# A hybrid decoder layer: the output projection of a tile placed inside the index work of the next

## The reference, cut to what matters

```python
scores = sum_h w_idx[h] * relu(q_idx[h] @ k_idx.T)      # 8 index heads
sel    = top_k(scores where valid, 256)                 # per query
att    = softmax(q @ k[sel].T / 8) @ v[sel]             # 8 heads of 64, 2 key/value heads
mo     = softmax(q_mem @ mem_k.T / 8) @ mem_v           # 4 heads, 256 memory tokens
o      = concat(att * silu(g_att), conv * silu(g_conv), mo * silu(g_mem)) @ w_out
y      = x + rms_norm(o, g_post)
```

## Time and profile before

| what | us |
|---|---|
| median of 3 runs | 2714.32 (2706.91 to 2717.56) |
| the profiled execution | 2714.81 |
| its span | 2712.7 |
| stage B, tiles 0 to 15 | 729.7 to 2453.1 |
| tile 10, whole | 1701.2 to 1841.7 |

### The profile page before, as it was taken

How to read it: one execution, slowest core, us unless ns; L and a number is a source line. 1 busy time by engine, 2 the same in 40 slices (tenths; PEclk the granted TensorE clock), 3 DMA queues, 4 the chain that set the end, 5 groups by cost and what they waited for, 6 DMA issues and landing times.

```text
span 2712.7 us, 34490 instructions
## 1 busy us (share of the span) xinstructions
PE 2246.7 (83%) x12592; PEld 1777.6 (66%) x12592; DVE 1414.5 (52%) x3260; ACT 1022.6 (38%) x1849; POOL 318.7 (12%) x847
## 2 busy tenths in 40 slices
PE   7999999999487887977978678687878879898865
PEld 5777777777365665765766657475766668687762
DVE  2444444442445566287487566847673645133580
ACT  1111101110244464374574655556536544352000
POOL 0000000000012121122111111201101110001004
PEclk9999999998677677678888788778977978998556
DMA  6111111110511111011011010101000101113001
GB/s 254 64 71 68 60 56 69 64 54 22 188 49 57 55 57 49 10 55 49 11 55 33 24 49 9 49 8 33 9 18 24 34 8 34 49 63 132 2 1 32
DMA packets 58412, 137.56 MB, mean 51 GB/s; under 512 B 13904, under 2 KB 26872, under 8 KB 57248
## 3 DMA queue, kind: packets, MB, share of 16 engines
q1 hardware_dynamic: 56096, 125.25, 13.7%
q0 software_dynamic: 2176, 10.49, 1.2%
HBM read 96.82 MB, written 38.90 MB: 50 GB/s over the span
## 4 chain that ended last, share of the span: by engine, by line
PE 60%; DVE 18%; ACT 10%; issue 7%; DMA 2%; POOL 1%; SPq 1%; PEld 1%; DVEq 0%; ACTq 0%; POOLq 0%; PEldq 0%
PE psum L564 12%; PE psum L1273 9%; PE psum L1262 9%; PE psum L597 8%; PE psum L1254 5%; PE psum L1231 4%; DVE sb_sc L996 4%; PE psum L1244 4%; ACT sb_ajunk L898 4%; DVE sb_junk L1011 2%; PE psum L1220 2%; ACT sb_ptb L892 2%; ACT sb_p L952 1%; PE psum L611 1%; PE psum L1706 1%
## 5 line engine op out<-in xcount | busy, mean ns | idle before, releaser
L1262 PE MATMUL psum<-sb_v,sb_ptb 128*128 128x64 f32 x2176 | 335.2, 303 | 30.7 <-ACT sb_ptb L892 29.9
L1262 PEld LDWEIGHTS psum<-sb_v,sb_ptb 128*128 128x128 f32 x2176 | 321.1, 224 | 48.8 <-ACT sb_ptb L892 48.3
L564 PE MATMUL psum<-sb_w,sb_xt 128*128 128x512 f32 (+5 forms) x1088 | 324.7, 459 | 0.5 <-DVE sb_xt L380 0.5
L1011 DVE TENSOR_SCALAR_CACHE_REDUCE sb_junk<-sb_sc,sb_c 128x384 bf16<-128x384 f32 (+6 forms) x217 | 305.6, 1408 | 4.2 <-DVE sb_mix L1190 1.0
L1244 PE MATMUL psum<-sb_ks,sb_qa 128*128 128x512 f32 (+3 forms) x640 | 204.4, 458 | 119.4 <-ACT sb_p L942 77.0
L1254 PE MATMUL psum<-sb_con,sb_p 128*128 128x128 f32 x1280 | 250.4, 327 | 63.9 <-ACT sb_p L952 41.2
L898 ACT ACTIVATE sb_ajunk<-sb_sc,sb_an 128x512 int8<-128x512 f32 (+6 forms) x217 | 293.8, 1354 | 10.3 <-POOL sb_an L826 9.8
L892 ACT ACTIVATE sb_ptb<-psum 128x512 f32<-128x512 f32 (+3 forms) x352 | 182.9, 534 | 239.3 <-PE psum L1254 237.9
L1273 PE MATMUL psum<-sb_wo,sb_mix 128*128 128x512 f32 x512 | 258.5, 669 | 13.4 <-DVEq L1193 13.4
L564 PEld LDWEIGHTS psum<-sb_w,sb_xt 128*128 128x128 f32 (+1 forms) x1088 | 178.5, 185 | 134.5 <-issue 125.1
L1231 PEld LDWEIGHTS psum<-sb_qa,sb_w 128*128 128x128 f32 x2048 | 244.2, 192 | 12.1 <-issue 4.7
(11 more groups left out here) (340 smaller groups left out, 2490.3 us busy)
## 6 DMA issues: line engine op xcount, KB each, us to landing
qt_s<-sb_qt SPq DMA_DIRECT2D x32, 512.0 KB, 2.8
sb_x<-in_x_prompt SPq DMA_DIRECT2D x16, 512.0 KB, 3.7
xt_s<-sb_xt SPq DMA_DIRECT2D x16, 512.0 KB, 2.6
sb_qa<-xt_s SPq DMA_DIRECT2D x16, 512.0 KB, 3.3
sb_qa<-qt_s SPq DMA_DIRECT2D x16, 512.0 KB, 3.5
sb_qa<-qt_s SPq DMA_DIRECT2D x32, 256.0 KB, 4.7
sb_xres<-in_x_prompt SPq DMA_DIRECT2D x16, 512.0 KB, 4.8
out_y_prompt<-sb_y SPq DMA_DIRECT2D x16, 512.0 KB, 3.4
```

The source lines that it names most:

```text
L564: mm = pe.matmul(out, m.xt[:, p, k, 0:n], m.w1[:, k, lo:hi], start=(k == 0), stop=(k == KD - 1))
L1011: return dve.tensor_scalar(m.junk[:, 0:w], m.sc(i), least[:], 0.0, ALU.is_ge, ALU.add, accum_out=m.cnt[:])
L1262: mm = pe.matmul(o, m.ptb[:, g, x * P:(x + 1) * P], v, start=st, stop=sp)
```

## The change

A tile's index stretch becomes a list of 12 segments on each engine, and the loop runs one pass longer. Segments 0 to 7 hold one gate block each, those of the second half first. Segment 7 holds the transposes of the attention of the tile before (`ta`) and the memory scores; segments 8 to 11 hold the projection of the tile before in four quarters, bank 1 first; segment 10 also holds the scores of the tile's first head. The index pairs are spread over segments 0 to 10.

On ACT both halves of the gate's input are copied to SBUF (`z0`, `z1`) beside the exponentials; the logarithm and the second exponential follow in segment 7, behind `gated` of the tile before; the memory exponentials stand ahead of the relus of segment 8. In the heads the exponential of head h + 1 stands after the second take of head h, and probes after the takes.

On DVE the division of the attention opens the next tile's list. The select of an odd tile is cut in three (segments 2, 4, 5), that of an even tile in three too (heads 5 to 7). Of the searches in a tile with index work, 2 (even j) or 7 (odd j) stand in the segments and the rest in the heads. The projection is read bank by bank: ACT squares each half, DVE multiplies each half by `gpost` (`gains`), and the scale and the residual follow in one instruction on DVE in head 2 (`residual`); POOL's addition is gone. The rows `junk` and `equal`, the latter a source of the sum in `select`, become 8-bit. `xt2` has its own buffer; `m.r` lies in a part of `p`.

On SP the second index tile's queries are issued after half of the gate weights, and the queries of a tile right behind the last scores of the tile before.

The core of the diff (of the loops, only what stands there after):

```diff
 AHEAD = 4
-Y_AFTER = 3
+SEGS = 12
+GATE_ORDER = (4, 5, 6, 7, 0, 1, 2, 3)
...
+def units(j, x):
+
+    if not searched(j + AHEAD):
+        return []
+    every = [(c, hp) for c in chunks(width(j + AHEAD), 512) for hp in range(4)]
+    return [u for k, u in enumerate(every) if k * (SEG_SCORE + 1) // len(every) == x]
...
+def searches_early(j):
+
+    return (2 if j % 2 == 0 else 7) if searched(j + AHEAD) else (4 if j % 2 == 0 else 8)
+
+
+def due(x, n):
+
+    return (x + 1) * n // SEG_SCORE > x * n // SEG_SCORE if x < SEG_SCORE else False
...
+    def load_xt(j):
+        if j >= 1:
+            sp.wait_ge(s.t_done, turns.of[("z", j - 1, 0)][1])
+        sp.dma_start(m.xt2.rearrange("p k n -> p (k n)"), io.xt_s[j]).then_inc(s.xt2_ld, 16)
+
     load_idx(FIRST)
-    for k in range(KD):
-        w = io.w_in[0, k * P:(k + 1) * P, :]
-        sp.dma_start(m.w2[:, k, 0:512], w[:, W2A[0]:W2A[1]]).then_inc(s.w_ld[k], 16)
-        sp.dma_start(m.w2[:, k, 512:1024], w[:, W2B[0]:W2B[1]]).then_inc(s.w_ld[k], 16)
+    load_xt(0)
+    for x, (lo, hi) in ((1, W2B), (0, W2A)):
+        for k in range(KD):
+            sp.dma_start(m.w2[:, k, 512 * x:512 * x + 512], io.w_in[0, k * P:(k + 1) * P, lo:hi]
+                         ).then_inc((s.w_ld, s.w_ldb)[x][k], 16)
+        if x == 1:
+            load_idx(FIRST + 1)
+    load_q(m.qa, 0, 0, s.qa_ld)
...
+        for x in range(SEGS):
+            if 0 <= j < NT and x == SEG_MEM + 1:
+                slot = scores.of[("M", j)][0]
+                act.wait_ge(s.mmax, j + 1)
+                for h in range(NMH):
+                    ins = act.activation(m.pm[:, h * 256:(h + 1) * 256], m.score2(slot)[:, mem_at(h) * 256:][:, 0:256],
+                                         ACT.Exp, bias=m.mnb[:, mem_at(h):mem_at(h) + 1], scale=SCALE,
+                                         accum_out=m.ml[:, h:h + 1])
+                ins.then_inc(s.mem_exp, 1)
+            for c, hp in units(j, x):
+                relu(j + AHEAD, c, hp)
+            if not 0 <= j < NT:
+                continue
+            if x == 3:
+                slot, n, _, _ = turns.of[("z", j, 1)]
+                act.wait_ge(s.t_done, n)
+                if j >= 1:
+                    act.wait_ge(s.gsum, j)
+                    act.wait_ge(s.t_dve, turns.of[("to", j - 1)][3])
+                act.activation(m.z1[:], m.turn[slot][:], ACT.Copy)
+                act.activation(m.gate[:, 512:768], m.turn[slot][:, 256:512], ACT.Exp, scale=-1.0).then_inc(s.zact, 1)
+            if x == SEG_MEM:
+                slot, n, _, _ = turns.of[("z", j, 0)]
+                act.wait_ge(s.t_done, n)
+                if j >= 1:
+                    act.wait_ge(s.gated, j)
+                act.activation(m.z0[:], m.turn[slot][:], ACT.Copy)
+                act.activation(m.gate[:, 0:512], m.turn[slot][:], ACT.Exp, scale=-1.0).then_inc(s.zact, 1)
+                act.wait_ge(s.zact, 2 * j + 2)
+                act.activation(m.gate[:], m.gate[:], ACT.Ln, bias=m.ones[:]).then_inc(s.zln, 1)
+                act.wait_ge(s.zln, 2 * j + 1)
+                act.activation(m.gate[:], m.gate[:], ACT.Exp, scale=-1.0).then_inc(s.zln, 1)
+            if its and due(x, probes_early(j)):
+                probe(j, its[done])
+                done += 1
+        if j >= 1:
+            square(j - 1, 1)
+            square(j - 1, 0)
+        if not 0 <= j < NT:
             continue
         for x in range(2):
             take_group(("tm", j, x))
+        exponent(j, 0)
         start = done
         for h in range(NH):
+            parts = chunks(width(j), 512)
+            for x, c in enumerate(parts):
+                take_group(("t", j, h, c))
+                if x == min(1, len(parts) - 1) and h + 1 < NH:
+                    exponent(j, h + 1)
             upto = start + (len(its) - start) * (h + 1) // NH
...
+    def select(i, c, part):
+        bias, e, run = m.bias[:, i % 2, 0:w], m.equal[:, 0:w], sc[:, 0:w // 2].bitcast(BF16)
+        if part == 0:
+            ch.inc(dve.tensor_scalar(c[:], c[:], sign, None, ALU.mult))
+            ch.link(dve.tensor_scalar(sc, sc, sign, None, ALU.mult))
+            ch.link(dve.tensor_scalar(bias, sc, c[:], 0.0, ALU.is_gt, ALU.add, accum_out=m.cnt[:]))
+            ch.inc(dve.tensor_scalar(m.more[:], m.cnt[:], -float(TOPK), None, ALU.add))
+            ch.link(dve.tensor_scalar(e, sc, c[:], None, ALU.is_equal))
+        if part == 1:
+            ch.link(dve.tensor_tensor_scan(run, e, m.one[:].to_broadcast([P, w]), m.more[:], ALU.add, ALU.min))
+        if part == 2:
+            ch.link(dve.scalar_tensor_tensor(out=e, in0=run, scalar=0.0, in1=e, op0=ALU.is_le, op1=ALU.mult))
+            ch.link(dve.tensor_tensor(bias, bias, e, ALU.add))
+            ch.link(dve.tensor_scalar(bias, bias, 1.0, MASK, ALU.subtract, ALU.mult))
...
+        half = slice(512 * x, 512 * x + 512)
+        dve.tensor_tensor(m.y[:, half], m.ybank[:, half], m.gpost[:, half], ALU.mult).then_inc(s.y_norm, 1)
...
+        dve.scalar_tensor_tensor(out=m.y[:], in0=m.y[:], scalar=m.yrs[:], in1=m.xres[:], op0=ALU.mult,
+                                 op1=ALU.add).then_inc(s.y_sum, 1)
...
+        if j >= 1:
+            attended(j - 1)
+        for x in range(SEGS):
+            acc = [(j + AHEAD, c, 2 * hp + e) for c, hp in units(j, x) for e in range(2)]
+            if d is not None and due(x, searches_early(j)):
+                search(d, done, acc)
+                done += 1
+            else:
+                for a in acc:
+                    accumulate(*a)
+            if j < 0:
+                continue
+            if j % 2 == 0 and 1 <= n < NPAIR:
+                if x == 0:
+                    exact(2 * n + 1)
+                if x in (2, 4, 5):
+                    select(2 * n + 1, m.cf, (2, 4, 5).index(x))
+            if j >= 1 and x == SEG_MEM:
+                gated(j - 1)
+                if j == NT:
+                    decode = c_prepare(dve, m, s)
+            if j == NT:
+                continue
+            if x == SEG_MEM:
+                slot, num, _, _ = scores.of[("M", j)]
+                dve.wait_ge(s.s_done, num)
+                ch.link(dve.tensor_reduce(m.mmx[:], m.score2(slot).rearrange("p (h n) -> p h n", h=NMH), AX, ALU.max))
+                dve.tensor_scalar(m.mnb[:], m.mmx[:], -SCALE, None, ALU.mult).then_inc(s.mmax, 1)
+            if x == SEG_MEM + 2:
+                dve.wait_ge(s.zln, 2 * j + 2)
+                ch.inc(dve.tensor_tensor(m.gate[:, 0:512], m.z0[:], m.gate[:, 0:512], ALU.mult))
+                ch.link(dve.tensor_tensor(m.gate[:, 512:768], m.z1[:, 256:512], m.gate[:, 512:768], ALU.mult))
+                dve.sem_inc(s.gsum, 1)
+            if x == SEG_SCORE:
+                for part in range(3):
+                    mask(j, 0, part)
...
+        for h in range(1, NH):
+            heads = 4 if j % 2 == 1 else NH - 1
+            target = min(upto, start + ((upto - start) * h + heads - 1) // heads)
...
+                if j >= 1:
+                    residual(j - 1)
...
+            if h >= 5 and d is not None and j % 2 == 1:
+                select(d, m.c, h - 5)
...
+    for j in range(FIRST - AHEAD, NT + 1):
         i = j + AHEAD
+        if searched(i):
             pe.wait_ge(s.qi_ld, 48 * (i + 1 - FIRST))
+        for x in range(SEGS):
+            if 0 <= j < NT and x < 8:
+                if x == 0:
                     pe.wait_ge(s.xt2_ld, 16 * (j + 1))
+                gate_block(j, GATE_ORDER[x])
+            if j >= 1 and x == SEG_TURN:
+                pe.wait_ge(s.att, j)
+                turn_group(("ta", j - 1), m.att, 0, 4)
+            if j >= 1 and x >= 8:
+                if x == 8:
+                    pe.wait_ge(s.cm_ld, 16 * j)
+                    pe.wait_ge(s.t_dve, turns.of[("to", j - 1)][3])
+                    if j == 1:
+                        pe.wait_ge(s.wo_ld, 32)
+                if x == 9:
+                    pe.wait_ge(s.gated, j)
+                mm = project_out(1 if x < 10 else 0, x % 2 == 0)
+                if x % 2 == 1:
+                    mm.then_inc(s.y_done, 1)
+            for c, hp in units(j, x):
+                index_pair(i, c, hp)
+            if 0 <= j < NT and x == SEG_MEM:
+                memory_scores(j)
+            if 0 <= j < NT and x == SEG_SCORE:
+                pe.wait_ge(s.qa_ld, 48 * (j + 1))
+                for h in range(first_scores(j)):
+                    scores_of(j, h)
...
-            m.r = sb(b, "r", [P, 2, 512])
-            m.junk = sb(b, "junk", [P, SEQ], BF16)
+            m.junk = sb(b, "junk", [P, SEQ], mybir.dt.uint8)
...
+            m.r = m.p[:, 1, 1024:2048].rearrange("p (e n) -> p e n", e=2)
...
+            m.xt2 = sb(b, "xt2", [P, KD, P])
+            m.gate = sb(b, "gate", [P, 768])
+            m.z0, m.z1 = sb(b, "z0", [P, 512]), sb(b, "z1", [P, 512])
+            m.equal = m.z0[:].bitcast(mybir.dt.uint8)
```

422 lines of the change are left out of this document (163 added, 259 removed).

## The result

| kernel | median, us | runs | ratio to before, 95% interval |
|---|---|---|---|
| before | 2713.53 | 2706.91 to 2717.56 | 1 |
| changed | 2497.76 | 2496.64 to 2500.80 | 0.9209 (0.9189 to 0.9229) |

The forecast was 2480, 18 us less than measured. The profiled execution of the changed kernel has a span of 2494.7 us, 218.0 less than the 2712.7 before.

The account below looks back on a forecast made before the run. DVE's busy time was taken as the floor in tiles 4 to 13: 760.9 + 10 × (1.4 + 17 + 6) = 1004.9 against 1202.1, −197. With −28, −10, −4 and +4: −235, so 2480 us, range 2375 to 2630.

Parts of the forecast that it names:

- the 8-bit row: DVE's select: the sum reading the 8-bit `equal` row may slow; +4 us taken, between 0 and +8.9 over 14 selects.
- E: Tiles 4 to 13: DVE's idle time per tile beside its busy floor, waiting on uncovered chains; 17 us.
- (a): End of the heads: DVE's division waits for the last head's exponential, turns and values; 7.7 us per tile, bounds 4 and 9.5.
- (b): Gate chain, started only behind `gated` of the tile before, counted whole as DVE idle time; 6.1 us per tile, lower bound 0.
- (c): Remainder for a tile's first index pair and the squares ahead of the gains; 3.2 us per tile, between 0 and 6.1.
- the clock: Heads: 2 of 7 per tile fall to PE's lower clock at 3 us each; 6 us per tile, from none to +11 more.
- rival D: Heads: PE's lower clock holds through all of them, making the kernel slower, +328 us to 2808; chance 0.06.
- A: Overlap better than forecast: PE stays fed with its clock up (−60) and less DVE idling (−25), 2395 us; chance 0.13.
- B: Index stretch: the gate and memory chain blocks ACT, stopping PE's pairs and DVE; +10 us in eleven tiles, 2590; chance 0.15.
- C: Whole kernel: the change does not do what it says, only the start's and small gains; about 2700 us; chance 0.06.
- the first relu: Sign in the index stretch: DVE's wait for a tile's first relu falls from 182.3 us to a few per tile.
- PE's wait for the memory exponentials: Sign: this wait, 77.0 us before, falls below 20 us; staying at tens of us would mean B.

Follow-up runs that it names:

- half a projection: The changed kernel with 16 of the 32 output projection matmuls of each tile left out; 2441.29 us.
- the older order: The changed kernel with ACT's order in the heads as before the change: exponential, one probe, the takes, further probes; 2477.07 us.
- 2465.19: The changed kernel with 10 of a tile's 15 or 16 DVE searches in the index segments, instead of 2 or 7; 2465.19 us.
- 2438.84: The changed kernel with some searches moved from the heads to the tile's start, around the attention division; 2438.84 us.
- four edits: The changed kernel with searches at the tile's start, 16-bit equal row, ACT's head order as before, and 4 or 9 early searches; 2446.27 us.
- one that did nothing alone: Memory scores, row maximum and exponentials moved to segments 5 and 6: 2497.45 us on the changed kernel, 2417.56 us added to the four edits.
- head order by width: The changed kernel with searches first, 16-bit equal row, memory softmax early, and another ACT head order in tiles 12 to 15; 2457.59 us.

## Why the prediction was right, point by point

**What bounds.** Right for the heads, too simple for the tile. The two engines took turns, and the projection was the largest piece: undone alone, it takes back 182 of 216 us. That DVE sets the heads afterwards is shown by the run without searches (−133). That DVE's whole list is the floor isn't shown: in tiles 8 to 11 all of half a projection came back, most of it in the index stretch, so there PE sets the time. The prediction put PE aside because its busy time would be 764 us at full clock, but that is above the 760.9 of DVE, not below; and after the change PE is still the busier engine, 891.6 us against 787.1. DVE's busy time and its idle time always add up to the whole, so that the sum came out doesn't show that DVE bounds it.

**The terms of the sum.** The two profiled executions, each term as forecast and as measured:

| term | forecast | measured |
|---|---|---|
| start of the tiles | −4 | −5.0 (729.7 to 724.7) |
| tiles 0 to 3 | −28 | −33.8 (259.1 against 308.9 less a projection of 16.05) |
| tiles 4 to 13, the 8-bit row in it | −193 | −162.7 (1039.4 against 1202.1) |
| tiles 14 and 15 with the last projection | −10 | −15.0 (213.5 against 212.4 and 16.05) |

The miss is in tiles 4 to 13, 1039.4 us for 1008.9; the other terms gave 12 us more than forecast and hid part of it. DVE's busy time there is 787.1 us, where 760.9 + 14 + 4 gave 778.9. The 8-bit row is one part of that: I took the middle of its bounds, and the sum's time (1757 ns) came out at the upper one, 4.9 us more over the 14 selects. The rest is what stands between: 1039.4 − 787.1 = 252.3 us, 25.2 per tile, where 17 + 6 = 23 were forecast. The range isn't made of the terms named beside it: 2480 less 60 and 60 is 2360, and with 110 and 9 more it is 2599; 2375 and 2630 don't follow from them.

**E, piece by piece.** (a) The end of the heads: 52.4 + 7.2 = 59.6 us in ten tiles, 6.0 each for 7.7. (b) The gate chain: the first accumulate behind it waits 4.5 to 6.3 us in tiles 4 to 11 (6.29 in tile 10), 44.1 in all; tiles 12 and 13 have no accumulates. That is 4.4 per tile for 6.1. (c) The remainder and the clock, 3.2 + 6 = 9.2, came out at 25.2 − 6.0 − 4.4 = 14.8. This is the term that was too small, by 56 us over ten tiles, and its make-up was wrong. It holds the first relu of a tile (31.0 us in all, 2.77 of them at 1569.42 in tile 10), relus later in the segments (32.3), masks (24.3), the gains (19.5), 13.5 us of smaller waits, and 28 us of short gaps that the view of waits doesn't list.

**Luck.** That 2480 lies so near the result is in part luck. (c) without the clock was forecast at 3.2 us and came out near 15; the 6 us for the clock, meant for something else, filled half of that hole, and the 1.7 us per tile that (a) and (b) each had too much filled another part. Without the clock's 60 us the same account would have said 2420.

**The clock.** The 6 us for it were no term of their own. Tile 10's heads fell to the lower level (a granted clock of 0.50) twice, about as often as forecast (2 of 7 heads). From 1656.1 to 1662.9 us DVE was busy through it, so nothing was paid. From 1680.0 on it took the last head:

```profile
1683.97 3.09 PE L1339 MATMUL psum<-sb_v,sb_ptb 128*128 128x64 f32 x14
```

Eight such matmuls take 1.00 us at full clock. DVE waits for these values, and this is a part of its 7.98 us at the division, so the clock's price stands in (a). With the searches out, the clock of the heads was 1.00. The rule of the Trainium skill on bursts ("TensorE: Matmul & The Clock Gate", section "HAM oscillation — how this bites in real kernels"), behind the slower rival D, agrees with the trace only so far: bursts between waits did fall to the lower level here, but in tile 10 for two heads of eight, not for all. D's condition, 72% of the heads at the lower level, would be a mean clock of about 0.64 in them by an estimate from the two levels; tile 10 had 0.88 and tile 11 0.82.

**The rivals.** A (2395) fell because DVE sets the heads. B (2590) was half right in its mechanism: the chain of gate and memory softmax still holds up PE for 37.5 us and DVE for 6.3 in tile 10, but at 4.5 to 6.3 us per tile, which E held already. C fell.

**Signs named ahead.** Right: the first relu (182.3 to 61.2 us, though later relus took some of it over), the normalisation, DVE's share (75.7%, just over the 75), the clock in the heads (0.88). Wrong: PE's wait for the memory exponentials fell to 37.5 us and not below 20, which by the prediction's own list spoke for B; the prediction had read the 77.0 as a wait for the turns, and it is one for the score slot. And PE's largest wait is not for masks or softmaxes but for the takes (57.2). The exponential that was put ahead stands in front of the next take on ACT; with the older order that wait was 36.2, while PE's wait for the head softmax rose from 33.7 to 48.4.

**Costed at nothing.** The earlier exponentials: in tiles 0 to 11 that held, within about 3 us. The searches' place: I took DVE's list as a whole and so did not see that the odd tiles' heads were over-filled; 2465.19 and 2438.84 show it, with most of their gain in odd tiles.

## What to carry to other kernels

Where two engines take turns, add up each one's busy time for the whole period, and forecast from one of the sums plus the waits of that engine's own list; here it came within 1% of the new time, though some terms were wrong and offset each other. Then do the same for each stretch, and ask which engine ends it: DVE ended the heads, PE most of the index stretch in tiles 8 to 11. Work of the bounding engine that stands in the wrong stretch (9 or 13 searches in the heads, none in the 8 us at the tile's end) was worth another 59 us. Gains measured one by one need not add up: four edits gave 51 us together, where one of them alone gave 59, and one that did nothing alone gave 29 on top of them.

## What the runs showed of the hardware

- A sum of two rows on DVE took 1757 ns at width 1536 when one of them was 8-bit, and 957 ns when both were 16-bit (959 when the row was made 16-bit again); the product into an 8-bit row (1747) cost what the 16-bit one did (1757).
- The same matmuls of tiles 12 and 13 ran at a mean granted clock from 0.85 to 0.98 depending on how ACT's and DVE's lists were arranged around them. In tile 13 PE was busy 98.6 us at 0.86 and 86.2 at 0.98, 12 of the 17 us by which the tile's time differed; the rest is PE's waiting. These two kernels, the head order by width and the older order alone, kept their whole time from run to run (2452.8 to 2459.3 and 2469.3 to 2479.5 us).
- Without DVE's searches, PE held a clock of 1.00 over 44 us of heads while 95% busy.
